# A decoder layer on one core: a second load of x moved behind a weight load, a gather cut in halves, expert ranks by pairs, a last weight block by columns

## Time and profile before

| | |
|---|---|
| median of 3 runs (lowest, highest) | 1605.92 us (1605.64, 1607.27) |
| the profiled execution | 1606.35 us |
| its span, first to last instruction | 1604.5 us |
| busy share of the span: PE, DVE, ACT, POOL | 83%, 42%, 13%, 2% |
| chain that ended last | DMA 53%, PE 41%, DVE 3% |
| moved by the DMA engines | 609.83 MB, mean 380 GB/s |

### The profile page before, as it was taken

The page is one execution under the profiler, slowest core; times in us unless marked ns, Lnnn a source line. Parts: engine busy times, 40 slices in busy tenths (PEclk is TensorE's granted clock), DMA queues, the critical chain, the costliest instruction groups (busy, mean ns, idle before and its releaser), DMA issues.

```text
span 1604.5 us, 18063 instructions
## 1 busy us (share of the span) xinstructions
PE 1335.1 (83%) x7501; PEld 804.9 (50%) x7501; DVE 666.7 (42%) x852; ACT 202.5 (13%) x502; POOL 28.7 (2%) x32
## 2 busy tenths in 40 slices
PE   6999999999999989989667677678767767767867
PEld 5767888888988858744123123223223213223223
DVE  5768686887676777241121121121122112112212
ACT  3001222221132111211001001001001001001001
POOL 0000000000010000100000000000000000000000
PEclk9999999999999999999788888887788888787879
DMA  9999687856875796999999999999999999999997
GB/s 394 426 425 383 254 328 301 329 220 253 320 307 220 313 374 272 391 405 424 428 428 428 429 428 428 429 428 428 428 429 429 428 428 429 429 428 429 428 429 294
DMA packets 45257, 609.83 MB, mean 380 GB/s; under 512 B 4976, under 2 KB 5504, under 8 KB 6944
## 3 DMA queue, kind: packets, MB, share of 16 engines
q1 hardware_dynamic: 44000, 604.26, 90.1%
q0 software_dynamic: 784, 4.34, 0.7%
q10 hardware_dynamic: 432, 0.65, 0.1%
HBM read 607.13 MB, written 2.10 MB: 380 GB/s over the span
## 4 chain that ended last, share of the span: by engine, by line
DMA 53%; PE 41%; DVE 3%; ACT 1%; issue 1%; SPq 0%; POOL 0%; ACTq 0%; DVEq 0%; POOLq 0%
DMA ring<-in_exp_w 35%; PE W L684 19%; DMA Zpad<-in_exp_w 9%; DMA ring<-in_stream 6%; PE M L1102 5%; PE W L661 3%; DMA tail<-in_exp_w 3%; PE W L985 2%; PE A L1120 2%; PE W L1054 2%; DVE ring L1467 1%; PE W L1067 1%; PE W L638 1%; PE W L1011 1%; PE M L1074 1%
## 5 line engine op out<-in xcount | busy, mean ns | idle before, releaser
L1102 PE MATMUL M<-ring,g1b 128*32 128x512 f32 x1280 | 183.4, 704 | 76.7 <-DMA ring<-in_exp_w 76.5
L1467 DVE CUSTOM_DVE_ANT_0 ring<-ring,tail 128x2048 f32<-128x2048 f32 x96 | 221.3, 2349 | 47.1 <-DMA ring<-in_stream 47.1
L1413 DVE TENSOR_TENSOR consts<-A,tail 32x512 f32<-32x512 f32 x128 | 87.8, 686 | 159.9 <-PE A L1120 156.9
L2011 DVE SCALAR_TENSOR_TENSOR tail<-tail,M 128x128 f32<-128x128 f32 x32 | 9.2, 288 | 299.3 <-ACT tail L1390 299.3
L1102 PEld LDWEIGHTS M<-ring,g1b 128*32 128x32 f32 x1280 | 38.9, 119 | 186.3 <-DMA ring<-in_exp_w 113.5
L684 PE MATMUL W<-ring,buf_x 128*128 128x256 f32 x576 | 128.9, 380 | 0.5 <-DVE ring L1413 0.5
L684 PE MATMUL W<-ring,buf_h 128*128 128x256 f32 x576 | 128.7, 380 | 0.0
L684 PEld LDWEIGHTS W<-ring,buf_x 128*128 128x128 f32 x576 | 108.4, 190 | 16.4 <-DVE ring L1413 0.9
L684 PEld LDWEIGHTS W<-ring,buf_h 128*128 128x128 f32 x576 | 108.6, 190 | 15.4 <-issue 1.1
L1074 PEld LDWEIGHTS M<-consts,tail 128*128 128x128 f32 x512 | 66.6, 203 | 93.2 <-ACT tail L1392 60.3
L1120 PE MATMUL A<-Zpad,tail 128*32 128x512 f32 x512 | 85.1, 795 | 29.3 <-DMA Zpad<-in_exp_w 22.5
(11 more groups left out here) (331 smaller groups left out, 1403.8 us busy)
## 6 DMA issues: line engine op xcount, KB each, us to landing
ring<-in_exp_w SPq DMA_DIRECT2D x96, 2048.0 KB, 36.6
ring<-in_stream SPq DMA_DIRECT2D x86, 2048.0 KB, 13.0
Zpad<-in_exp_w SPq DMA_DIRECT2D x56, 2048.0 KB, 38.0
PPY<-in_exp_w SPq DMA_DIRECT2D x24, 2048.0 KB, 30.6
tail<-in_exp_w SPq DMA_DIRECT2D x16, 2048.0 KB, 45.4
Zpad<-in_early SPq DMA_DIRECT2D x16, 1024.0 KB, 19.5
buf_x<-in_x SPq DMA_DIRECT2D x2, 1024.0 KB, 6.3
buf_h<-in_x POOLq DMA_DIRECT2D x1, 2048.0 KB, 19.7
```

What stands on the lines that cost most here:

```text
L1102: ins = pe.matmul(M[32 * j:32 * j + 32, 512 * w13:512 * w13 + 512], XT[:, kk, 32 * q:32 * q + 32], w[:, 512 * k:512 * k + 512], start=(kk ...
L1413: return dve.tensor_tensor(o, x, y, op)
L1467: ins = dve.tensor_tensor_reduce(w, w, c_rows[:], 1.0, first[:, j:j + 1], ALU.mult, ALU.add, to[:, j:j + 1])
```

## The change

It has these parts.

- **Second load of x.** POOL waits, ahead of this load, until half 77 (the second of block 1) has landed. The loads of `wr` and `rb` and the power for mixer r stay behind it in POOL's order.
- **First residual sum.** `residual(0)` comes after sums_24 of out1, and multiplies in place in PSUM; ACT's square sums of that part move behind four of out1's corner copies.
- **Block 3 by columns.** Its two halves are now 256 columns by all 2048 rows, in place of 512 columns by 1024 rows, so that each of PE's two steps needs one half and frees it.
- **Diagonals of g2** are made between the fourth and the fifth residual part, and the wait of half j = 9 is for g2's row sums and the square sums in place of g2's copies.
- **Ranks by pairs.** The second and further steps of the two `first_maximum` calls over 8 experts give way to comparisons of all pairs of 8 (128 elements a row), a sum over them, and a comparison with 2. The two single choices are made later, behind the mask.
- **Gather in halves.** `gather(hf)` makes two of the four blocks. The first expert of a group takes its halves in the order w1, w3 (first half of rows), `gather(1)`, w1, w3 (second half); SP loads them in that order. The gather ahead of the fourth expert only makes the first half, for the next group.
- **POOL's clearing of `ysb`** waits for `g_ready` in place of `router_done`.

```diff
@@ SP: experts' halves
             def expert_half(g, j):
                 q, part, hf = j // 6, j % 6 // 2, j % 2
+                if (q, part) in ((0, 0), (0, 1)):
+                    part, hf = hf, part
...
                 elif j == 9:
-                    sp.wait_ge(sem["g2_ready"], 1)
+                    sp.wait_ge(sem["x1_squared"], 5)
+                    sp.wait_ge(sem["g2_summed"], 1)
@@ POOL
                     item_done(pool, 'chunk', arg)
+                    i = STREAM.index(('wout', 1, 1))
+                    pool.wait_ge(slot_full[i % RING], 16 * (i // RING + 1))
                     pool.dma_start(x1, a['x'][0].rearrange("(a p) d -> p a d", p=P)).then_inc(sem["x_again"], 16)
...
             pool.wait_ge(sem["gt_ready"], 1)
-            pool.wait_ge(sem["router_done"], 1)
+            pool.wait_ge(sem["g_ready"], 1)
@@ PE: block 3
-                    w0 = half_arrives()
-                    half[0] += 1
-                    w1 = half_arrives()
-                    half[0] += 1
                     for c in range(2):
+                        w = half_arrives()
                         for kk in range(KT):
-                            w = w0 if kk < 8 else w1
                             for tt in range(TT):
                                 p0 = o + 512 * c + 256 * tt
-                                p1 = 512 * (kk % 8) + 256 * c
-                                ins = pe.matmul(W[:, p0:p0 + 256], YT[:, kk, tt * P:tt * P + P], w[:, p1:p1 + 256],
+                                ins = pe.matmul(W[:, p0:p0 + 256], YT[:, kk, tt * P:tt * P + P],
+                                                w[:, 256 * kk:256 * kk + 256],
                                                 start=(kk == 0 and tt == 0), stop=(kk == KT - 1), skip_group_check=True)
+                        half_done(ins)
                         if c == 0:
-                            ins.then_inc(sem["wout_part"], 1)
                             turn_x1(2, range(8, 12))
                             router_wide(1)
-                        else:
-                            ins.then_inc(half_used, 2)
@@ PE: gather and first expert
-            def gather():
-                for b in range(4):
+            def gather(hf):
+                for b in range(2 * hf, 2 * hf + 2):
...
             pe.wait_ge(sem["g2_ready"], 1)
-            gather()
-            pe.wait_ge(sem["g_ready"], 1)
+            gather(0)
             rounds = load_rounds(pe)
...
-                            gather()
-                        for w13 in range(2):
-                            for hf in range(2):
-                                if (q, w13) == (0, 0):
-                                    pe.wait_ge(sem["xt_act"], 2 * it + (hf + 1))
-                                    pe.wait_ge(sem["xt_dve"], 2 * it + (hf + 1))
+                            gather(0)
+                        for i in range(4):
+                            w13, hf = (i % 2, i // 2) if q == 0 else (i // 2, i % 2)
+                            if (q, i) == (0, 2):
+                                pe.wait_ge(sem["g2_ready"], 2)
+                                gather(1)
+                            if q == 0 and w13 == 0:
+                                pe.wait_ge(sem["xt_act"], 2 * it + (hf + 1))
+                                pe.wait_ge(sem["xt_dve"], 2 * it + (hf + 1))
...
-                                if (w13, hf) == (1, 0):
+                            if i == (3 if q == 0 else 2):
...
+                                sum_and_turn(h1T).then_inc(sem["h_turned"], 1)
@@ ACT: first expert of a group
+                        if q == 0:
+                            dress_tokens(it, 1)
+                        act.wait_ge(half_used, PER_GROUP * it + (PE_BASE + 6 * q + (3 if q == 0 else 2)))
                         act.activation(part, M[:, 0:512], ACT.Copy).then_inc(sem["part_copied"], 1)
                         act.wait_ge(sem["h_turned"], 8 * it + (2 * q + 1))
+                        if q == 0:
+                            act.wait_ge(sem["g_ready"], it + 1)
                         act.activation(ee, h1T, ACT.Tanh, scale=0.5).then_inc(sem["e_ready"], 1)
@@ DVE: residual
                 width = d.stop - d.start
-                t3 = tmp[:, 0:TT * width].rearrange("p (a d) -> p a d", a=TT)
+                w3 = w_ap.rearrange("p (a d) -> p a d", a=TT)
+                t3 = w3 if n == 0 else tmp[:, 0:TT * width].rearrange("p (a d) -> p a d", a=TT)
...
             for n in range(3):
-                if n == 0:
-                    item_done(dve, 'wout', n)
-                    residual(n, W[:, 1024:2048], slice(0, 512))
-                else:
+                if n > 0:
                     corners(f'out{n}')
                     residual(n, tmp[:, 0:1024], slice(512 * n, 512 * n + 512))
                 if n < 2:
                     sums_24(f'out{n + 1}')
                 if n == 0:
+                    item_done(dve, 'wout', n)
+                    residual(n, W[:, 1024:2048], slice(0, 512))
                     scale_router()
...
             residual(3, W[:, 0:512], slice(1536, 1792))
+            dve.wait_ge(sem["ada_half_used"], halves_used(EXPERT_BASE)[1])
+            diagonals(g2_diag, g2_cols).then_inc(sem["diag_ready"], 1)
             item_done(dve, 'wout', 3)
             residual(4, W[:, 512:1024], slice(1792, 2048))
-            dve.wait_ge(sem["ada_half_used"], halves_used(EXPERT_BASE)[1])
-            diagonals(g2_diag, g2_cols).then_inc(sem["diag_ready"], 1)
@@ DVE: ranks
-            first_maximum(o1, lev, rt[:, 2:4], EPG)
-            dve.scalar_tensor_tensor(l2, o1, NEG, lev, ALU.mult, ALU.add).then_inc(sem["dve_step"], 1)
-            dve.wait_ge(sem["dve_step"], step_no())
-            first_maximum(o2, l2, rt[:, 4:6], EPG)
+            tt_op(level, lev_i, lev_j, ALU.is_equal).then_inc(sem["dve_step"], 1)
+            tt_op(above, lev_i, lev_j, ALU.is_gt)
+            dve.wait_ge(sem["dve_step"], step_no())
+            tt_op(level, level, ahead.unsqueeze(1).to_broadcast(pairs), ALU.mult).then_inc(sem["dve_step"], 1)
+            dve.wait_ge(sem["dve_step"], step_no())
+            tt_op(above, above, level, ALU.add).then_inc(sem["dve_step"], 1)
+            dve.wait_ge(sem["dve_step"], step_no())
+            dve.tensor_reduce(rank, above, AX, ALU.add).then_inc(sem["dve_step"], 1)
+            dve.wait_ge(sem["dve_step"], step_no())
             both = w12.rearrange("p (a j) -> p a j", a=TT)
-            tt_op(both, o1, o2, ALU.add).then_inc(sem["dve_step"], 1)
+            dve.tensor_scalar(both, rank, 2.0, None, ALU.is_lt).then_inc(sem["dve_step"], 1)
```

More of the change, by code:

```diff
@@ L439, in build_program @@
         jdesc = tmp[:, 1760:1792]
+        ahead = tmp[:, 1280:1344].rearrange("p (j i) -> p j i", j=EPG)
+        above, level = (tmp[:, 768 + 128 * i:896 + 128 * i].rearrange("p (a j i) -> p a j i", a=TT, j=EPG) for i in range(2))
         w12 = tmp[:, 1792:1808]
@@ L1188, in copy_corner @@
                     act.wait_ge(half_used, halves_used(halves_of(name)[int(i == 4)] + 1)[0])
-                if i == 0 and name[:3] == 'out':
-                    act.wait_ge(sem["x1_ready"], int(name[3:]))
+                if (name, i) == ('out2', 0):
+                    act.wait_ge(sem["x1_ready"], 2)
                 if i == 3 and s > 0 and name != 'out2':
@@ L1340, in keep_turned @@
                 act.activation(Z[:, k0 * T:k1 * T], M[:, o:o + (k1 - k0) * T], ACT.Copy).then_inc(sem["xT_copied2"], 1)
+            for i in range(4):
+                copy_corner('out1', i)
             square_sums(0, slice(0, 512))
-            for i in range(5):
-                copy_corner('out1', i)
+            copy_corner('out1', 4)
             keep_turned(0, 0, 4)
@@ L1365, in _, with dress_tokens @@
                 ins = act.activation(g2c[32 * m:32 * m + 32, :], W[32 * m:32 * m + 32, 512 * m:512 * m + 512], ACT.Copy)
-            ins.then_inc(sem["g2_ready"], 1)
+                if m % 2 == 1:
+                    ins.then_inc(sem["g2_ready"], 1)
+            def dress_tokens(n, hf):
+                act.wait_ge(sem["gathered"], 4 * n + (2 * hf + 1))
+                for k in range(8 * hf, 8 * hf + 4):
+                    ins = act.activation(XT[:, k, :], W[:, k * P:k * P + P], ACT.Identity,
+                                         scale=gsc[:, KT + k:KT + k + 1],
+                                         bias=modc[:, 3 * KT + k:3 * KT + k + 1])
+                ins.then_inc(sem["xt_act"], 1)
+            dress_tokens(0, 0)
             act.wait_ge(sem["group_arg"], 1)
@@ L1396, in _ @@
                         if q == 3:
-                            for b in (0, 2):
-                                act.wait_ge(sem["gathered"], 4 * it + (b + 5))
-                                dress_tokens(b)
+                            dress_tokens(it + 1, 0)
         @block.vector
@@ L1942, in _, with dress_tokens @@
             tt_op(Gm, column(pos3, 0), iob, ALU.is_equal).then_inc(sem["first_ready"], 1)
```

(27 more changed lines are left out.)

71 lines of the change are left out of this document (28 added, 43 removed).

## The result

The changed kernel is slower: median 1619.78 us of 6 runs (1617.98 to 1623.20) beside 1606.35 us of 6 runs of the kernel before, ratio 1.0079 with a 95% interval of 1.0067 to 1.0091. The prediction said 1618.3 us. The profiled execution took 1619.36 us, its span 1617.5.

The account below looks back on a forecast made before the run. Bound: PE leaving the output projection, then the first group up to half j = 17, after which DMA streams unbroken. 10.3 - 1.1 + 3.2 = 12.4 us later on the profiled 1606.35, less 0.4 to the median: 1618.3 us; range 1613.5 to 1623.

Parts of the forecast that it names:

- The hold: POOL's wait for half 77 delays mixer r's power to 581.0 and PE's turn to 583.7 instead of 568.32: +15.4 us.
- The restart: Block 0's second half on PE, after the long stand, runs slower: +1.6 us, bounds 0 and 3.3.
- PE's wait for out2's sums: Output projection: half 81 lands late, at 622.5, so PE waits +0.6 us.
- Out of block 3: PE's end of the output projection's last block: 15.4 + 1.6 - 5.3 - 1.6 + 0.6 - 0.4 = +10.3 us.
- The gather started: Router: ACT frees half of W first, so the gather, which waited for ACT, starts 1.1 us earlier.
- The way from the gather to the first w2: First group: dressing waits after each half gather, +3.0, and w3's sums copy, +0.2; bounds -0.1 to +6.5 us.
- The last term: Last w2, scatter, add and store behind the last load: 15.4 us, left alone by the change.
- the stand goes: Out1 on PE: with the residual moved, both sums_24 come in time; stand and restart vanish, -5.3 and -1.6 us.
- (A): Rival: POOL's power is not held, or 77 lands before PE needs r's output; 1601.4 us, chance 0.05.
- (B): Rival: the first group doesn't set the stream, the release of half j = 10 does; +6.2, 1612.1 us, chance 0.07.
- (C): Rival: POOL's clearing holds the dressing, or PE restarts twice in the first expert; about 1622 us, chance 0.14.
- the columns: Output projection's last block by columns removes PE's wait for its second half: -0.4 us.

Follow-up runs that it names:

- e3: Kernel before plus only POOL's wait for half 77 ahead of the second load of x; ratio 1.0083 to the kernel before.
- e10: Kernel before plus only POOL's wait ahead of the second load of x, but for half 76 instead of 77; ratio 1.0045 to the kernel before.
- e2: Changed kernel with POOL's wait and second load of x moved behind the power for mixer r; ratio 0.9968 to the kernel before.
- e9: Kernel before with only the second load of x and a wait for half 77 behind the power of mixer r; ratio 0.9972.
- e6: e2 with the first residual sum back ahead of sums_24 of out1 and ACT's square sums ahead of its corner copies; ratio 0.9980 to the kernel before.
- e1: Changed kernel without POOL's wait for half 77, all else kept; ratio 0.9987 to the kernel before, median 1605.73 us.
- e4: Changed kernel with both halves of the gather one behind the other on PE, all else kept; ratio 1.0053 to the kernel before.
- e5: e2 with the edit of e4 (power first and gather whole); ratio 0.9958 to the kernel before, median 1602.78 us.
- e7: e5 with the first expert's halves in the old order again (both of w1, then w3); ratio 0.9947 to the kernel before.
- e8: e5 with the two experts found by the old `first_maximum` steps instead of ranks by pairs; ratio 0.9971 to the kernel before.

## Why the prediction was right, and where it was off

It was right in its main step, by its own mechanism. **The hold:** 77 down at 577.0 (said: 576.8), the power done at 581.1 (581.0), PE's turn at 583.74 (583.7), +15.4 as said. e3 shows that this wait alone makes the loss, e10 that the loss goes with the length of the hold, e2 that it is the place in POOL's order: with the power first, POOL waits as long and nobody loses. By the Trainium skill (DMA: Bandwidth & Descriptors, Anatomy of one DMA) the sequencer that issues a DMA does its waiting, not the DMA engines; the trace agrees, POOL's power starting at 579.43 us, behind the three issues.

**Terms that were mis-sized.** The restart was taken as 1.6 and was 17.57 - 15.42 = 2.15 us (block 0 done at 600.50 instead of 582.93), inside its bounds. PE's wait for out2's sums was taken as 0.6 and was 1.29, as half 81 was in DVE's hands at 623.62 and not at 622.5 (for DVE's last 3.76 us of standing ahead of it the chain shows no releaser, only "issue"; that it was this half is read from DVE's order). Out of block 3 PE came 11.4 later, not 10.3. The gather started 1.30 earlier relative to that (said 1.1). The way from the gather to the first w2 became 2.27 longer, not 3.2: the two stands were 1.65 and 1.64 (1.5 each said), but the 9.01 us of gather had held a restart, which was only named as a bound; the pieces took 3.84 each. And one term was missing: the first w2 at the lower clock (0.54 from 714.5 to 718.0 us), 1.37. The sum: 11.4 - 1.3 + 2.3 + 1.4 = 13.8 for the 13.7 measured at j = 17, against the 12.4 forecast. The last term, the 15.4 us behind the last load, was taken to stay and became 14.1: that load ends at 1603.43, 14.3 later than before, but the last w2 behind it took 1.97 us instead of 3.29. So the span came out 13.0 longer, nearer to the 12.4 than j = 17 did; that part is luck.

**One step had the right size and the wrong cause.** "Both sums_24 follow PE's first products, 2.3 us each, before it needs them: the stand goes" was written as the work of the moved residual. e3 keeps the residual in its place and the stand goes too, since PE is late; e9 and e6 keep it and the stand goes since the stream is free of x; e1, with the residual moved and x early, still has 2.79 us of it.

**The rivals.** (A) needed r's output by 573 us; it came at 583.7. What it would have been worth, 1601.4 on 1605.92 or a ratio of 0.9972, was measured when e2 took the hold away: 0.9968. (B) fell: the stream paused ahead of j = 17 (share 0.38 from 736.0 to 742.4 us), and e4 turned 3.8 us of first group into some 4 us of time. (C) fell in the trace: the dressing took 1.37 us beside the clearing, and of the two restarts in the first expert neither came behind the dressings (granted clock 1.00 from 693.0 to 707.6 us); what came was the 1.37 at the first w2. That the columns are worth 0.4 agrees with the 0.35 us that block 3 by rows waits in e3; by itself this was not tried.

## What to carry to other kernels

A wait in front of a load on an engine that also computes holds everything behind it in that engine's order: list those instructions and their users before you add it, and put the load last. When a load is not urgent, look at what shares the stream with it; here delaying one 2 MB load past a more urgent one, which also let a smaller load out early, gained 0.3%, and the same delay in the wrong place cost 0.8%.

## What the runs showed that was not expected

The price of a restart depended little on how long PE stood: 1.6 to 2.8 us for stands of 1.96 to 15.46 us. Behind stands of 0.78 to 1.29 us the next 32 matmuls took 7.17 us; behind 1.96 us (e6), 2.73 (e5) and 2.79 (e1) they took 8.86, that is 1.7 more, with a granted clock of 0.80 and 0.81 in those stretches; behind 5.27 us (before) 8.80; behind 10.29 us (e10) the turn and the 32 matmuls lost 0.93 + 1.85 = 2.8, behind 15.46 us (e3) 0.93 + 0.91 = 1.8. So in e5 a half that reached DVE 1.85 us later than in e2 went with 3.6 us of PE's time (1.86 of stand, 1.69 of restart). Single executions of one kernel differ by more than that, those of e1 from 1601.95 to 1611.49 us; whether such restarts make this spread is not shown, as one execution of each kernel was profiled.

The stretch at the lower clock in the first group also moves rather than goes. It lay in the gather before (9.01 us for what takes 7.41 in e4), in the first w2 in the change, e2 and e4, in the scatter behind it in e7 (5.40 us), in both of these in e1 and e5, and in all three in e8. What decides its place was not settled.
